# Fifteen of twenty 256 x 512 transposes of a two-layer mixer trunk moved from TensorE to VectorE block transposes and GpSimd copies

## The chip, the cores and the metric

One core of one Trainium2 chip runs the whole kernel in one launch. The metric is the device time of an execution in microseconds; lower is better. The kernel before has a median of 1819.05 us over three runs (1818.07 to 1819.42).

## What is computed

Two layers over x of 256 rows by 2048 columns, all in fp32. Cut to what matters here, a layer is:

```
h = rms_norm(x, norm_g)
p_sb, p_mla, p_rw, p_gate = split_cols(h @ w_in, ...)
y_sb  = stick_breaking_attention(...) * silu(sg)      # 256 x 512
y_mla = chunk_causal_softmax_attention(...) * silu(mg) # 256 x 1024
y_rw  = rwkv7_mixer(...) * silu(rg)                    # 256 x 512
g_sb, g_mla, g_rw = split_cols(sigmoid(p_gate), ...)   # 256 x 2048 each
merged = g_sb * (y_sb @ w_br_sb) + g_mla * (y_mla @ w_br_mla) + g_rw * (y_rw @ w_br_rw)
x = x + merged @ w_out
```

Every `@` with a weight needs its left operand with the columns on the partitions. So between the stages h, the gated branch outputs y and `merged` have to be transposed: per layer y in four pieces of 256 x 512, merged in four, and the new x in four before the next layer.

## The kernel before, in words

**Dense work.** The weights stream from HBM in chunks of 256 rows by up to 512 columns (0.5 MB), 280 chunks a layer in the fixed order of `GROUPS` (line 132). A chunk goes through four steps: SyncE loads it into one of four slots of `ring`; ScalarE (ACT) rounds it to `w_hi`; VectorE (DVE) writes the rest, `w_lo` = ring - w_hi; TensorE (PE) does twelve matmuls of 128 x 512 on it (hi x hi, hi x lo, lo x hi, for two halves of the rows and two blocks of 128) into one pair of the PSUM banks `D` (line 578). `LEAD` = 3: ACT and DVE split three chunks ahead of the one PE multiplies. `END[name]` is the number of chunks of a layer that are done when the group `name` ends; the groups near the change end at rg 184, gate11 192, mg0 200, mg1 208, sg 216, br0 218, bm0 222, bs0 224, then eight chunks for each next br/bm/bs trio, and o0 to o3 at 256, 264, 272 and 280.

**Order.** Every engine runs a program written out by hand. `dense_to(n)` emits an engine's share of the dense work up to chunk n, `beat()` the dense work up to the next step of the attention or RWKV work, which is laid between the chunks. Nothing is rescheduled: an engine that waits holds all that is behind it. DVE's share of the dense work holds the splits to `w_lo` and, in `take_out`, what becomes of a group's banks: the gating by SiLU (`rg`, `mg`, `sg`, which multiply `xy`), the merge (`br`, `bm`, `bs`, which build `MJ`) and the residual (`o`, which adds to `xy`).

**Transposes.** The four pieces of y are transposed by PE (line 632, function `transposes`) at `AT_RW` = mg1 + 2 chunks (the RWKV piece and the first MLA piece), `AT_ML1` = mg1 + 4 and `AT_SB` = after br0; the four pieces of merged by line 867 at `merged_at(j)`, three chunks after bs_j; the new x by line 632 at `renewed_at(j)`, two chunks after o_j, with the fourth piece two chunks into the next layer. A piece is eight transposes of 128 x 128 into two banks `B`. ACT then writes the rounded hi part from the bank and DVE the lo part, and PE's later matmuls wait for those (`br_dve`, `mt_dve`, `xt_dve`). With four pieces of y and four of merged in each layer, and four of x between the layers, that is twenty pieces.

**GpSimd (POOL)** masks the RWKV levels and the stick-breaking weights (`affine_select`, line 551, which PE waits for), spills the gates to HBM and reads them back three at a time (line 564), each read waiting until DVE has used the buffer.

## Time and profile before

| | |
|---|---|
| median of three runs | 1819.05 us |
| the profiled execution's own time | 1821.68 us |
| its span in the trace | 1819.9 us |
| granted TensorE clock, mean over the span | 0.997 of full speed |
| instructions | 22316 |
| HBM traffic over the span | 183 GB/s |

The profile is of one execution. Its times are from the span's start. "Busy" counts time in which an instruction of the engine runs; a matmul's end is modelled, so PE's next start says more than the duration of one. A line such as L1195 or L887 is that of a helper used for many things: the tile names tell them apart.

### The profile page before, as it was taken

The numbers are of one execution on the slowest core, as the hardware profiler recorded it, in microseconds if no ns is written. First come the engines' busy times: TensorE is split into PE (matmuls) and PEld (weight loads), VectorE is DVE, ScalarE is ACT, GpSimd is POOL, SyncE is SP. The second block draws the span as 40 slices with busy tenths as digits, with TensorE's granted clock in tenths as the row PEclk, the third lists the DMA queues.
The fourth block names the chain that finished last, engine by engine and source line by source line (L and its number), as shares of the span: only waits on it lengthen the run. The fifth ranks groups of instructions, "written<-read, shape, count | busy, mean of one in ns | idle before, by whom it ended". The sixth has DMA issues, their size and how long they took to land.

```text
span 1819.9 us, 22316 instructions
## 1 busy us (share of the span) xinstructions
PE 1778.6 (98%) x8912; PEld 1498.6 (82%) x8912; DVE 1074.2 (59%) x1388; ACT 880.7 (48%) x1234; POOL 138.9 (8%) x159
## 2 busy tenths in 40 slices
PE   6899999999999999999999999999999999999998
PEld 5678888889888888788888788888888888887887
DVE  3568454554866645686556774645557656467753
ACT  4444444334454666455544444434344555765532
POOL 1010111211000000100000010201100000001000
PEclk9999999999999999999999999999999999999999
DMA  7865555445565554785677655546456555558754
GB/s 235 237 192 177 173 159 165 149 143 170 174 187 154 165 152 153 258 281 181 208 231 236 188 164 154 170 139 183 135 168 193 160 159 159 150 174 309 238 188 155
DMA packets 178943, 335.19 MB, mean 184 GB/s; under 512 B 22556, under 2 KB 35258, under 8 KB 178168
## 3 DMA queue, kind: packets, MB, share of 16 engines
q1 hardware_dynamic: 169816, 297.67, 53.7%
q0 software_dynamic: 9024, 36.10, 5.6%
q8 instruction: 70, 1.15, 0.3%
q14 instruction: 33, 0.27, 0.0%
HBM read 313.56 MB, written 18.87 MB: 183 GB/s over the span
## 4 chain that ended last, share of the span: by engine, by line
PE 87%; DMA 4%; DVE 3%; ACT 3%; issue 1%; SPq 1%; ACTq 0%; DVEq 0%
PE D L578 73%; PE B L578 11%; DMA ring<-in_w_in 2%; DMA ring<-in_w_br_rw 2%; ACT arena L887 1%; DVE w_lo L1195 1%; DVE arena L1195 1%; ACT L887 1%; ACT w_hi L887 1%; PE B L632 0%; DVE xy L1195 0%; PE B L648 0%; PE B L867 0%; DMA xy<-in_x 0%; DVE gev L1233 0%
## 5 line engine op out<-in xcount | busy, mean ns | idle before, releaser
L1195 DVE TENSOR_TENSOR w_lo<-ring,w_hi 128x1024 fp32r<-128x1024 f32 (+3 forms) x560 | 661.7, 1195 | 457.0 <-ACT w_hi L887 448.5
L887 ACT ACTIVATE w_hi<-ring 128x1024 fp32r<-128x1024 f32 (+3 forms) x560 | 572.9, 1037 | 388.1 <-PE D L578 279.8
L578 PE MATMUL D<-w_hi,ht_hi 128*128 128x512 f32 (+2 forms) x1728 | 692.0, 400 | 16.4 <-DVE w_lo L1195 13.3
L578 PE MATMUL D<-w_hi,ht_lo 128*128 128x512 f32 (+2 forms) x1728 | 668.4, 387 | 0.0
L578 PE MATMUL D<-w_lo,ht_hi 128*128 128x512 f32 (+2 forms) x1728 | 666.8, 386 | 0.0
L578 PEld LDWEIGHTS D<-w_hi,ht_hi 128*128 128x128 f32 x1728 | 326.7, 189 | 80.4 <-DVE w_lo L1195 15.9
L578 PEld LDWEIGHTS D<-w_hi,ht_lo 128*128 128x128 f32 x1728 | 325.8, 189 | 67.3
L578 PEld LDWEIGHTS D<-w_lo,ht_hi 128*128 128x128 f32 x1728 | 327.0, 189 | 57.2 <-issue 0.5
L578 PEld LDWEIGHTS B<-arena 128*128 128x128 f32 (+3 forms) x1568 | 205.2, 190 | 24.6 <-issue 7.6
L578 PE MATMUL B<-arena 128*128 128x128 f32 (+5 forms) x1568 | 220.3, 293 | 1.4 <-DVE arena L1369 1.1
L887 ACT ACTIVATE arena<-B 128x512 f32<-128x512 f32 (+4 forms) x168 | 81.0, 491 | 286.7 <-PE B L578 229.3
L578 PE MATMUL D<-w_hi,mt_lo 128*128 128x512 f32 x256 | 100.5, 393 | 0.0
L578 PE MATMUL D<-w_hi,mt_hi 128*128 128x512 f32 x256 | 100.4, 392 | 0.0
L578 PE MATMUL D<-w_lo,mt_hi 128*128 128x512 f32 x256 | 100.1, 391 | 0.0
L526 POOL TENSOR_TENSOR arena<-arena,con 128x512 f32<-128x512 f32 x48 | 74.1, 1544 | 338.1 <-DVE arena L1308 185.8
L1195 DVE TENSOR_TENSOR arena<-arena,B 128x512 f32<-128x512 f32 x48 | 33.0, 687 | 59.5 <-PE B L578 59.5
L517 POOL DMA_DIRECT2D gate_spill<-gev x24 | 17.8, 743 | 636.9 <-ACT gev L887 636.9
L887 ACT ACTIVATE arena<-B,small 128x256 f32<-128x256 f32 (+1 forms) x48 | 20.8, 436 | 94.2 <-DVE small L1374 50.2
L887 ACT ACTIVATE arena<-arena 128x1024 f32<-128x1024 f32 (+4 forms) x72 | 54.0, 749 | 23.2 <-DVE small L1341 13.7
L1195 DVE TENSOR_TENSOR arena<-arena 128x1024 f32<-128x1024 f32 (+3 forms) x86 | 63.9, 751 | 1.8
L887 ACT ACTIVATE gev<-D,small 128x512 f32<-128x512 f32 (+1 forms) x64 | 40.4, 680 | 40.2 <-PE D L578 40.1
L578 PEld LDWEIGHTS D<-w_lo,mt_hi 128*128 128x128 f32 x256 | 48.1, 188 | 10.7
(135 smaller groups left out, 1276.7 us busy)
## 6 DMA issues: line engine op xcount, KB each, us to landing
ring<-in_w_in SPq DMA_DIRECT2D x368, 512.0 KB, 3.9
ring<-in_w_out SPq DMA_DIRECT2D x64, 512.0 KB, 4.8
ring<-in_w_br_mla SPq DMA_DIRECT2D x32, 512.0 KB, 4.7
gate_spill<-gev POOLq DMA_DIRECT2D x24, 512.0 KB, 4.2
arena<-gate_spill POOLq DMA_DIRECT2D x24, 512.0 KB, 4.9
ring<-in_mla_w_ukv SPq DMA_DIRECT2D x16, 512.0 KB, 4.1
ring<-in_w_br_rw SPq DMA_DIRECT2D x16, 512.0 KB, 6.4
ring<-in_w_br_sb SPq DMA_DIRECT2D x16, 512.0 KB, 5.3
```

What stands on the lines that cost most here:

```text
L517: pool.dma_start(spill[n].rearrange("(h p) c -> p h c", p=P), gev[:, n % 2, :, :]).then_inc(spilled[n % 2][l], 16)
L526: nc.gpsimd.tensor_tensor(LM, AM[:, :, 0:P], level[n].unsqueeze(1).to_broadcast([P, 4, P]), ALU.mult).then_inc(rw_pool, 1)
L578: return nc.tensor.matmul(o, a, b, start=start, stop=stop, skip_group_check=True)
L887: return nc.scalar.activation(o, i, fn, **kw)
L1195: return v.tensor_tensor(o, a, b, op)
```

## The change

For 15 of the 20 pieces, all but the stick-breaking piece and merged's fourth in each layer and x's fourth, PE's eight transposes go. In their place:

- **DVE** does one block transpose (`turn_blocks`) of the whole piece right after it has written it: each 32 x 32 block is transposed in place of itself, from `xy` or `MJ` into a new buffer `TURN` of 128 x 1024. The wait in front of it is for its own write, and for POOL to have emptied `TURN`.
- **POOL** then moves blocks between the four quarters of 32 partitions (`move`): sixteen `tensor_copy` of 32 partitions x 256 elements, four at a time with a wait behind each four, into `ROUND`. Three moves stand around the stick-breaking pairs, three between the gate reads, three at the end of layer 0.
- **ACT and DVE** read the hi and lo parts from `ROUND` in SBUF where they read banks `B`; ACT waits for `rows_moved`. `merged_at(j)` is now five chunks after bs_j (it was three), for j = 0 to 2, and `renewed_at(j)` four after o_j (it was two).

```diff
 def merged_at(j):
-    return END[f"br{j + 1}"] + 1 if j < 3 else END["bs3"] + 4
+    return END[f"bs{j}"] + (5 if j < 3 else 4)
 def renewed_at(j):
-    return END[f"o{j}"] + (2 if j < 3 else 0)
+    return END[f"o{j}"] + 4
...
+        TURN = [PV.rearrange("p h c -> p (h c)")[:, 0:1024]]
+        ROUND = [[PV.rearrange("p h c -> p (h c)")[:, (1 + n) * 1024:(2 + n) * 1024] for n in range(2)]]
...
+        def round_of(q):
+            return ROUND[q >= 3][q % 2].rearrange("p (k t) -> p k t", k=4)
...
+                def move(q):
+                    pool.wait_ge(blocks_turned[l], q + 1)
+                    turned = TURN[q >= 3].rearrange("p (h k j t) -> p h k j t", h=2, k=4, j=4)
+                    moved = round_of(q).rearrange("p k (h i t) -> p h k i t", h=2, i=4)
+                    for d in range(4):
+                        for i in range(4):
+                            j = (i + d) % 4
+                            nc.gpsimd.tensor_copy(moved[32 * j:32 * j + 32, :, :, i, :],
+                                                  turned[32 * i:32 * i + 32, :, :, j, :]).then_inc(quadrants[l], 1)
+                        pool.wait_ge(quadrants[l], 16 * q + 4 * d + 4)
+                    pool.sem_inc(rows_moved[l], 1)
...
                 dense_to(END["sv"])
+                move(0)
                 for q in range(SBH // 2):
...
+                    if q == 0:
+                        move(1)
                 dense_to(END["gate11"])
+                pool.wait_ge(br_dve[l], 2)
+                move(2)
...
+                    if n >= 5 and n % 3 == 2:
+                        j = n // 3 - 1
+                        if j:
+                            pool.wait_ge(mt_dve[l], 2 * j)
+                        move(3 + j)
+                for j in range(3 if l + 1 < DEPTH else 0):
+                    if j:
+                        pool.wait_ge(xt_dve[l], 2 * j)
+                    else:
+                        pool.wait_ge(mt_dve[l], 6)
+                    move(6 + j)
...
-                dense_to(AT_RW)
+                dense_to(AT_SB)
                 pe.wait_ge(sb_dve, 8 * l + 8)
-                pe.wait_ge(silu_dve[l], 6)
-                transposes((0, 1), 1536, br_pe[l])
-                transposes((2, 3), 512, br_pe[l])
-                dense_to(AT_ML1)
-                pe.wait_ge(br_dve[l], 2)
-                transposes((4, 5), 1024, br_pe[l])
-                dense_to(AT_SB)
-                pe.wait_ge(br_dve[l], 4)
                 pe.wait_ge(silu_dve[l], 8)
                 transposes((6, 7), 0, br_pe[l])
...
+            def turn_blocks(q, block):
+                if q:
+                    dve.wait_ge(rows_moved[l], q)
+                v.transpose(TURN[q >= 3].rearrange("p (h c) -> p h c", h=2), block).then_inc(blocks_turned[l], 1)
...
                     tt(y, y, gev[:, n % 2, :, :], ALU.mult).then_inc(silu_dve[l], 2)
+                    if n < 3:
+                        dve.wait_ge(silu_dve[l], 2 * n + 2)
+                        turn_blocks(n, y)
...
                         v.sem_inc(merged[l], 1)
+                        if j < 3:
+                            turn_blocks(3 + j, MJ[:, j % 2, :, :])
...
                     v.sem_inc(dense_ev[l], 1)
+                    if l + 1 < DEPTH and j < 3:
+                        turn_blocks(6 + j, xy[:, :, j * 512:(j + 1) * 512])
```

What each engine now issues, at the three places that matter most. First DVE where group rg of layer 0 is taken out, in the middle of MLA head 6: `xy<-xy,gev` is the gating of the RWKV piece, and the COPY is the head's rotary part, which PE waits for. Before:

```order
L1233 SCALAR_TENSOR_TENSOR gev<-arena,small,gev 128x64
L1195 TENSOR_TENSOR xy<-xy,gev 128x2x512 [waits dense_out_0]
L1369 COPY arena<-B 64x512 [waits ml_pe]
L1195 TENSOR_TENSOR w_lo<-ring,w_hi 128x1024 [waits weights_hi]
L1372 TENSOR_REDUCE small<-B 128x1 [waits ml_pe]
```

and now:

```order
L1274 SCALAR_TENSOR_TENSOR gev<-arena,small,gev 128x64
L1230 TENSOR_TENSOR xy<-xy,gev 128x2x512 [waits dense_out_0]
L1258 STREAM_TRANSPOSE arena<-xy 128x1024 [waits silu_gated_0]
L1415 COPY arena<-B 64x512 [waits ml_pe]
L1230 TENSOR_TENSOR w_lo<-ring,w_hi 128x1024 [waits weights_hi]
L1418 TENSOR_REDUCE small<-B 128x1 [waits ml_pe]
```

The block transpose stands between the gating and the copy; the rest is in the order it had.

Second, POOL between the two stick-breaking pairs of layer 0 (the first pair's masks end, the second pair's begin); before, the four masks followed each other. Now:

```order
L576 AFFINE_SELECT arena<-arena 128x128 [waits sb_act]
L576 AFFINE_SELECT arena<-arena 128x128
L561 COPY arena<-arena 32x2x4x32 [waits blocks_turned_0]
L561 COPY arena<-arena 32x2x4x32 x3
L561 COPY arena<-arena 32x2x4x32 [waits quadrants_moved_0]
...
L576 AFFINE_SELECT arena<-arena 128x128 [waits quadrants_moved_0,sb_act]
L576 AFFINE_SELECT arena<-arena 128x128
```

The second pair's masks stand behind a whole move, and behind its wait for DVE's block transpose.

Third, DVE from the end of bs0 in layer 0: `arena<-arena 128x1024` is the last addition of merged's first piece, `mt_lo` its lo part. Before:

```order
L1195 TENSOR_TENSOR arena<-arena 128x1024 [waits dense_out_0]
L1195 TENSOR_TENSOR w_lo<-ring,w_hi 128x1024 [waits dve_order,weights_hi]
L1195 TENSOR_TENSOR w_lo<-ring,w_hi 128x1024 [waits weights_hi]
L1195 TENSOR_TENSOR arena<-arena,D 128x512 [waits ring_freed,gate_sigmoid_0]
L1195 TENSOR_TENSOR arena<-arena,D 128x512
L1195 TENSOR_TENSOR w_lo<-ring,w_hi 128x1024 [waits dense_out_0,weights_hi]
L1195 TENSOR_TENSOR mt_lo<-B,mt_hi 128x512 [waits merged_hi_0] x2
```

and now:

```order
L1230 TENSOR_TENSOR arena<-arena 128x1024 [waits dense_out_0]
L1258 STREAM_TRANSPOSE arena<-arena 128x1024 [waits dve_order,rows_moved_0]
L1230 TENSOR_TENSOR w_lo<-ring,w_hi 128x1024 [waits weights_hi] x2
L1230 TENSOR_TENSOR arena<-arena,D 128x512 [waits ring_freed,gate_sigmoid_0]
L1230 TENSOR_TENSOR arena<-arena,D 128x512
L1230 TENSOR_TENSOR w_lo<-ring,w_hi 128x1024 [waits dense_out_0,weights_hi]
L1230 TENSOR_TENSOR w_lo<-ring,w_hi 128x1024 [waits weights_hi] x2
L1230 TENSOR_TENSOR mt_lo<-arena,mt_hi 128x512 [waits merged_hi_0] x2
```

The block transpose comes ahead of two splits, the lo part comes two splits later, and its input is `ROUND` where it was a bank.

## Rows read from the trace of the kernel before

**Rows 1.** The page: busy time by engine, and the chain's shares.

```profile
PE 1778.6 (98%) x8912; PEld 1498.6 (82%) x8912; DVE 1074.2 (59%) x1388; ACT 880.7 (48%) x1234; POOL 138.9 (8%) x159
...
PE 87%; DMA 4%; DVE 3%; ACT 3%; issue 1%; SPq 1%; ACTq 0%; DVEq 0%
```

**Rows 2.** Groups by line and shape: count, busy us, mean ns, idle before.

```profile
L632 PE MATMUL B<-con,xy 128*128 128x128 f32 x128 | 19.9, 311 | 9.9 <-DMA xy<-in_x 9.9
...
L867 PE MATMUL B<-con,arena 128*128 128x128 f32 x64 | 8.3, 273 | 0.0
```

**Rows 3.** PE's timeline around merged's first piece: start us, us, instruction.

```profile
774.27 0.40 PE L578 MATMUL D<-w_hi,ckv_lo 128*128 128x512 f32 x1
774.51 1.04 PE L867 MATMUL B<-con,arena 128*128 128x128 f32 x8
775.30 0.48 PE L578 MATMUL D<-w_hi,ckv_hi 128*128 128x512 f32 x1
775.61 0.39 PE L578 MATMUL D<-w_lo,ckv_hi 128*128 128x512 f32 x1
775.84 0.40 PE L578 MATMUL D<-w_hi,ckv_lo 128*128 128x512 f32 x1
```

**Rows 4.** The chain that ended last, in order of time, over the same place.

```profile
774.67 0.87 PE B L867 x8
775.54 21.80 PE D L578 x96
797.35 0.87 PE B L867 x8
```

**Rows 5.** Groups by line and shape on DVE.

```profile
L1195 DVE TENSOR_TENSOR w_lo<-ring,w_hi 128x1024 fp32r<-128x1024 f32 x512 | 618.6, 1222 | 412.9 <-ACT w_hi L887 404.6 <-DVE arena L1195 2.0 <-DVE small L1524 0.3
...
L1195 DVE TENSOR_TENSOR arena<-arena,D 128x512 f32<-128x512 f32 x48 | 30.8, 684 | 9.2 <-ACT arena L887 4.4 <-PE D L578 3.8 <-issue 1.1
...
L1323 DVE STREAM_TRANSPOSE arena<-arena 128x512 f32<-128x512 f32 x32 | 22.8, 712 | 1.1
```

**Rows 6.** DVE's and PE's timelines where rg is taken out, layer 0.

```profile
631.50 1.23 DVE L1195 TENSOR_TENSOR xy<-xy,gev 128x1024 f32<-128x1024 f32 x1
632.64 0.67 DVE L1369 COPY arena<-B 64x512 f32<-64x512 f32 x1
...
633.46 0.90 PE L578 MATMUL B<-arena 128*128 128x128 f32 x5 [0.42 <-DVE arena L1369]
```

**Rows 7.** DVE's timeline from bs0's merge on, layer 0.

```profile
771.15 1.23 DVE L1195 TENSOR_TENSOR arena<-arena 128x1024 f32<-128x1024 f32 x1
772.62 2.36 DVE L1195 TENSOR_TENSOR w_lo<-ring,w_hi 128x1024 fp32r<-128x1024 f32 x2 [0.24 <-DVE arena L1195]
774.89 1.28 DVE L1195 TENSOR_TENSOR arena<-arena,D 128x512 f32<-128x512 f32 x2
```

**Rows 8.** Groups by line and shape on POOL.

```profile
L526 POOL TENSOR_TENSOR arena<-arena,con 128x512 f32<-128x512 f32 x48 | 74.1, 1544 | 338.1 <-DVE arena L1308 185.8 <-PE B L578 152.3
...
L551 POOL TENSOR_SCALAR_AFFINE_SELECT arena<-arena 128x128 f32<-128x128 f32 x16 | 4.2, 291 | 90.6 <-ACT arena L887 90.6
...
L493 POOL MEMSET arena<- 1x256 f32 x4 | 1.2, 304 | 0.2
...
L493 POOL MEMSET arena<- 128x128 f32 x2 | 0.4, 212 | 0.1
```

**Rows 9.** POOL's and DVE's timelines, where both want SBUF.

```profile
407.55 2.09 POOL L526 TENSOR_TENSOR arena<-arena,con 128x512 f32<-128x512 f32 x1 [1.92 <-PE B L578]
...
187.19 1.31 POOL L526 TENSOR_TENSOR arena<-arena,con 128x512 f32<-128x512 f32 x1 [3.59 <-PE B L578]
...
406.17 2.32 DVE L1195 TENSOR_TENSOR w_lo<-ring,w_hi 128x1024 fp32r<-128x1024 f32 x2
409.07 1.65 DVE L1195 TENSOR_TENSOR w_lo<-ring,w_hi 128x1024 fp32r<-128x1024 f32 x1 [0.58 <-ACT w_hi L887]
```

**Rows 10.** ACT at merged's first piece; DVE, ACT and PE at x's first piece.

```profile
775.69 1.07 ACT L887 ACTIVATE mt_hi<-B 128x512 fp32r<-128x512 f32 x2
776.64 1.06 ACT L887 ACTIVATE w_hi<-ring 128x1024 fp32r<-128x1024 f32 x1
...
857.48 1.28 DVE L1195 TENSOR_TENSOR xy<-xy,D 128x512 f32<-128x512 f32 x2 [0.45 <-PE D L578]
...
863.95 1.57 ACT L887 ACTIVATE ht_hi<-B,small 128x256 fp32r<-128x256 f32 x4
...
857.21 0.39 PE L578 MATMUL D<-w_hi,mt_hi 128*128 128x512 f32 x1
```

**Rows 11.** Busy us by engine, clock, DMA share, GB/s: the merge's first two groups.

```profile
775.30:798.00 22.70, 22.70 (x108) 18.88 (x106) 19.05 (x21) 12.86 (x15) 2.89 (x4) 1.00 0.90 309
798.00:820.66 22.66, 22.66 (x108) 18.85 (x105) 17.22 (x18) 12.31 (x14) 1.44 (x2) 1.00 0.75 258
```

**Rows 12.** The second stick-breaking pair: gating on DVE, masks on POOL, PE's use.

```profile
690.88 1.23 DVE L1195 TENSOR_TENSOR xy<-xy,gev 128x1024 f32<-128x1024 f32 x1
...
706.61 1.03 POOL L551 TENSOR_SCALAR_AFFINE_SELECT arena<-arena 128x128 f32<-128x128 f32 x4 [28.39 <-ACT arena L887]
...
709.80 1.50 PE L578 MATMUL B<-arena 128*128 128x128 f32 x12
```

More of the change, by code:

```diff
@@ L275, in program @@
         CQ, CKV = again(at_mkv, lambda: halved(1024), lambda: halved(1024))
+        turn, round_ = again(at_mkv, lambda: take(1024), lambda: take(1024))
+        TURN.append(turn)
+        ROUND.append([round_, round_])
         KR = halved(128)
@@ L845, in _ @@
                     sb_pair(q)
-                dense_to(AT_RW)
+                dense_to(AT_SB)
                 pe.wait_ge(sb_dve, 8 * l + 8)
-                pe.wait_ge(silu_dve[l], 6)
-                transposes((0, 1), 1536, br_pe[l])
-                transposes((2, 3), 512, br_pe[l])
-                dense_to(AT_ML1)
-                pe.wait_ge(br_dve[l], 2)
-                transposes((4, 5), 1024, br_pe[l])
-                dense_to(AT_SB)
-                pe.wait_ge(br_dve[l], 4)
                 pe.wait_ge(silu_dve[l], 8)
                 transposes((6, 7), 0, br_pe[l])
-                for j in range(4):
-                    dense_to(merged_at(j))
-                    pe.wait_ge(merged[l], j + 1)
-                    for s in range(2):
-                        if j:
-                            pe.wait_ge(mt_dve[l], 2 * j - 1 + s)
-                        for k in range(2):
-                            for h in range(HALVES):
-                                kk = 2 * s + k
-                                last = nc.tensor.transpose(B[s][:, k * 256 + h * P:k * 256 + (h + 1) * P],
-                                                           MJ[:, j % 2, h, kk * P:(kk + 1) * P], ident)
-                        last.then_inc(mt_pe[l], 1)
-                for j in range(3 if l + 1 < DEPTH else 0):
-                    dense_to(renewed_at(j))
-                    pe.wait_ge(x_new[l], j + 1)
-                    if j < 2:
-                        pe.wait_ge(mt_dve[l], 8)
-                    else:
-                        pe.wait_ge(xt_dve[l], 2 * j - 2)
-                    transposes((2 * j, 2 * j + 1), j * 512, xt_pe[l])
+                dense_to(merged_at(3))
+                pe.wait_ge(merged[l], 4)
+                for s in range(2):
+                    for k in range(2):
+                        for h in range(HALVES):
+                            kk = 2 * s + k
+                            last = nc.tensor.transpose(B[s][:, k * 256 + h * P:k * 256 + (h + 1) * P],
+                                                       MJ[:, 1, h, kk * P:(kk + 1) * P], ident)
+                    last.then_inc(mt_pe[l], 1)
                 dense_to(NCH)
@@ L1070, in sb_pair, with columns_hi @@
                 beat()
-            def columns_hi(j, ready, done):
+            def columns_hi(j, ready, done, before=0):
                 for s in (2 * j, 2 * j + 1):
-                    act.wait_ge(ready, s + 1)
+                    act.wait_ge(ready, s + 1 - before)
                     for i in range(2):
@@ L1079, in columns_hi, with renewed_hi @@
                     last.then_inc(done, 1)
+            def renewed_hi(j):
+                act.wait_ge(rows_moved[l], 7 + j)
+                for s in (2 * j, 2 * j + 1):
+                    for i in range(2):
+                        k = 2 * s + i
+                        last = f(hth[:, k, :], round_of(6 + j)[:, k % 4, :], scale=ng[:, k:k + 1])
+                    last.then_inc(xt_act[l], 1)
             def squares(j, done):
@@ L1428, in columns_lo, with renewed_lo @@
                     last.then_inc(done, 1)
+            def renewed_lo(j):
+                for s in (2 * j, 2 * j + 1):
+                    dve.wait_ge(xt_act[l], s + 1)
+                    for i in range(2):
+                        k = 2 * s + i
+                        last = v.scalar_tensor_tensor(htl[:, k, :], round_of(6 + j)[:, k % 4, :], ng[:, k:k + 1],
+                                                      hth[:, k, :].bitcast(F32), ALU.mult, ALU.subtract)
+                    last.then_inc(xt_dve[l], 1)
             def sum_squares(squared, done):
```

63 lines of the change are left out of this document (36 added, 27 removed).

## The prediction

> **What bounds the kernel now.** I read the page's busy times and the chain first [rows 1]. PE is busy 98% of the span and 87% of the chain that ended last is PE; DVE is at 59%, POOL at 8%. So an instruction taken off PE shortens the run, unless it stood in the shadow of a wait. The groups by line say whether the transposes did [rows 2]: before the 64 of line 867 PE never sat idle, and all 9.9 us before line 632 are waits for the input x at the start, which stay. The 120 transposes that go (15 pieces of eight) were therefore paid in full. Then I read the places where work is put in: DVE and PE around rg [rows 6], DVE after bs0 [rows 7], POOL between the stick-breaking pairs [rows 12], and the prices of what is added [rows 5, 8, 9].
>
> **What goes.** A transpose's row says 273 ns, but they overlap: eight run from 774.51, and the dense matmuls go on at 775.30, the next at 775.61 [rows 3]. From 774.27 to 775.61 are 1.34 us; two matmul intervals of 0.227 us (96 in 21.80 us [rows 4]) would have stood there anyway, which leaves 0.89 us for eight. The chain gives 0.87 twice [rows 4]. 15 x 0.89 = **13.4 us**. The stick-breaking piece, merged's fourth and x's fourth stay on PE, at no change.
>
> **What DVE gets.** Fifteen block transposes of 128x1024. The trace has them of 128x512, at 712 ns, beside 684 ns for an elementwise instruction of that size and 1222 ns for one of twice the size [rows 5]. By that slope a block transpose of twice the size takes 712 + 538 = 1.25 us, and 15 take 18.8 us of an engine with 41% idle. Where is one on the path?
> - *rg, once a layer.* PE waits 0.42 us for the COPY that DVE does right after the gating [rows 6]. The block transpose now stands between them. Nothing covers it: 1.25 us and 0.05 for the wait on the gating, twice = **+2.6 us**.
> - *bs0, once a layer.* DVE was held up by late weights here. Its pair of splits starts at 772.62, and the first of them, done at 773.84, is what PE's matmuls from 775.30 need [rows 3, 7]. Without the transposes PE wants it at 774.5; the block transpose (from 772.5 to 773.75) pushes it to 775.0. PE waits 0.5, twice = **+1.0 us**.
> - *Everywhere else* (mg0, mg1, bs1, bs2, o0 to o2) DVE works ahead of PE. In the group from bs1 to bs2 it is busy 17.2 of 22.66 us [rows 11]; with the block transpose 18.5 of the new 21.8. Cost 0; without that cover each would be 1.3 us.
>
> **What POOL gets.** Sixteen copies a piece, of 32 partitions x 256 elements. The trace has no POOL copy. Nearest below: a memset of 256 elements on few partitions, 304 ns. Nearest above with one input and one output: an affine select of 128 elements, 291 ns, twice that for 256 = 582 ns [rows 8]. From 128 to 256 elements a memset grows by 92 ns, so I take 291 + 92 = 383 ns for a copy, and keep both ends. The four waits of a move cost some 0.05 us each.
>
> POOL also gets in DVE's way and DVE in POOL's. A POOL instruction that takes 1.31 us alone took 2.09 when it met DVE's split of `w_lo`; the next split, which wanted to start while POOL was running, took 1.65 instead of 1.22 [rows 9]. So the two exclude each other while both read SBUF, and either may lose. The Trainium skill says the same (SBUF — State Buffer, "SBUF: two separate sides"): the shared port pair is an exclusive lock held for the whole instruction, against DVE instructions with two SBUF inputs too. By that rule, the trace agrees, all DVE splits and additions count, and the lo parts, which read a PSUM bank before and SBUF now, join them. During a move DVE has about two splits to do, 2.4 us. A move takes **T = 16c + 0.2 + 2.4**: 8.7 us at c = 0.383, 7.5 at 0.304, 11.9 at 0.582.
>
> Where does T reach PE? ACT waits for the moved rows, and with it the splits behind it; PE has three chunks in hand.
> - *Merged's first piece.* Turned at 773.75. After the move ACT's hi parts take 1.07 us, the next split 1.06 on ACT and 1.22 on DVE, the emptying of bm1's banks 1.28 [rows 5, 7, 10]: 4.6 us. PE wants that five chunks after 775.0, at 2.725 us a chunk (12 matmuls) = 788.6. T may be **10.2**.
> - *Merged's second and third.* Turned about 4.3 us after the next group starts (1.28 + 1.22 + 1.25 and 0.5 of waits), wanted 21.8 us after it: T may be **12.9**.
> - *x's pieces.* Turned at 857.48 + 1.28 + 1.35 = 860.1; then 1.57 + 1.06 + 1.22 + 0.1; wanted seven chunks of 2.745 after 857.21 = 876.4 [rows 10]. T may be **12.4**.
> - *The second stick-breaking pair.* The gating ends at 692.1, so the move starts at 693.4 and must be over, with 1.03 us of masks behind it, by PE's use at 709.80 [rows 12]: T may be **15.4**.
> - *The pieces of y.* rg's has 40 us to its use at mg1 + 2, mg1's has its use at the end of sg, some 16 us later.
>
> At 8.7 none is reached, and the move costs nothing but DVE's waits for POOL. Those count only where DVE is late, after bs0: between nothing and the four queued copies of a step (1.5 us) a layer. I take one copy, 0.4: **+0.8 us**.
>
> **Sum.** -13.4 + 2.6 + 1.0 + 0.8 = -9.0. The profiled execution took 1821.7, so 1812.7; the median of the runs is 2.6 lower than it, so **1810.1**. The bounds of the unknown terms: full gain (nothing lost at rg or bs0) -13.4, 1805.7; with the four queued copies (+2.2 more) and c at 0.582 (T 11.9, 1.7 over at merged's first piece, twice = 3.4) 1815.7.
>
> **Rivals.**
> 1. *The copies are slow, and the kernel gets slower.* For it: no row shows a copy between quarters of the partitions, and POOL's two-input instruction takes 1544 ns for 512 elements [rows 8], 0.77 for 256. At c = 0.77, T = 14.9: over the limit by 4.7 twice, 2.0 four times, 2.5 three times = 24.9 us; 1810.1 + 24.9 = 1835.0. Against it: a copy has one input, and part of the 1544 is waiting for DVE (1.31 undisturbed [rows 9]). It decides from T = 13.1, c = 0.66, where the stalls (5.8 + 0.8 + 2.1) eat the 9 us. The Trainium skill speaks for it (GPSIMD Engine Reference, "Key points"): only two of the eight cores reach all partitions, so such work runs at a quarter of the engine. If that quadrupled only the 92 ns per 128 elements, c would be 0.66, an estimate at the turning point itself. Chance 0.14.
> 2. *DVE becomes the bound in the merge.* 18.5 us of 21.8, and if it waits for all sixteen copies (6.1 us), 24.6: 2.8 over for six groups, less the some 5 us that each layer's three chunks in hand absorb: about 6.8 us. 1810.1 + 6.8 = 1816.9. For it: DVE did lose to POOL in rows 9; against it: it also won there. Chance 0.10.
> 3. *Weights, not PE.* The DMA of the chunks bounds the merge (309 and 258 GB/s in its first two groups [rows 11]), so that its six pieces give nothing: 1810.1 + 5.3 = 1815.4. Against: PE never idles there. Chance 0.05.
> 4. *rg costs nothing*, since PE waits elsewhere in the MLA chain anyway: 1807.5. Chance 0.08.
>
> Forecast as summed: 0.63.
>
> **Numbers.** Some 0.2% (3.6 us) is what a measurement of this kernel can tell from no change, so faster means under 1815.4. The forecast, the fourth rival and about half of the second and third lie there: 0.63 x 0.97 + 0.08 + 0.08 = 0.77. Same, up to 1822.7: the rest of those and a slow copy near the turning point: 0.11. Slower: 0.12. The range 1805.5 to 1818 takes in the bounds and rivals 2 to 4 and leaves out the slow copies, and a little on either side.
>
> **What would show it.** Right: transposes on PE down by 120; PE's gap at the COPY in MLA head 6 near 1.7 us instead of 0.42; a gap near 0.5 after bs0; the block transposes at 1.25 us; POOL's moves at 7 to 10 us, over before ACT reaches its read; groups of 21.8 us in the merge. Wrong: ACT's idle time before `mt_hi` put down to POOL with PE idle behind it (rival 1); `w_lo` well over 1.22 us and PE waiting for it in several groups (rival 2); ACT waiting for the ring with PE idle (rival 3).

## The result and the profile after

The changed kernel took 1825.84 us (median of five runs, 1822.58 to 1828.28), 1.0036 times the kernel before (95% interval 1.0024 to 1.0049). On another chip it took 1824.18 us (seven runs) beside 1819.60: 1.0027 (1.0016 to 1.0037). It is slower, by 4.6 to 6.8 us, where 9 us less were forecast.

The page of the changed kernel, against [rows 1]:

```profile
PE 1770.3 (97%) x8792; PEld 1486.0 (82%) x8792; DVE 1095.3 (60%) x1403; ACT 878.5 (48%) x1234; POOL 286.7 (16%) x399
...
PE 85%; DVE 6%; ACT 3%; DMA 3%; issue 2%; POOL 1%; SPq 0%; DVEq 0%; ACTq 0%; POOLq 0%
```

The transposes did go (120 instructions, 8.3 us of busy time), and POOL's busy time doubled; but DVE's share of the chain doubled too, and POOL appears in it. The groups by line on DVE and POOL, against [rows 5, 8]:

```profile
L1230 DVE TENSOR_TENSOR w_lo<-ring,w_hi 128x1024 fp32r<-128x1024 f32 x512 | 621.8, 1231 | 378.6 <-ACT w_hi L906 371.6 <-DVE arena L1230 0.5 <-DVE small L1579 0.3
...
L1258 DVE STREAM_TRANSPOSE arena<-xy 128x1024 f32<-128x1024 f32 x9 | 11.2, 1245 | 0.7
...
L561 POOL COPY arena<-arena 32x256 f32<-32x256 f32 x240 | 147.9, 616 | 136.2 <-DVE arena L1258 86.9 <-DVE cq_lo L1230 36.0
```

The block transpose takes 1.245 us, as forecast. A copy's mean of 616 ns is of two kinds: most take 0.39 us and some 1.3. Where TensorE waits is in the summary of its waits:

```profile
PE D L618 <- DVE arena L1230: 12.7, 8, 2.5
...
PE B L618 <- DVE arena L1415: 3.6, 2, 1.9
```

"arena" from line 1230 is the emptying of a pair of banks D. Eight long waits for it: one at br1 in each layer, which the kernel before has as well, and six new ones in the merge. Line 1415 is rg's COPY. The merge by windows, each from one group's first matmul to the next's (br1 to br2, to br3, to o0), against the 22.70 and 22.66 us of [rows 11]; the columns are us, busy us of PE, PEld, DVE, ACT and POOL with instructions in brackets, granted clock, DMA share, GB/s:

```profile
760.01:784.08 24.07, 22.35 (x97) 17.86 (x97) 18.52 (x20) 12.25 (x14) 12.94 (x19) 1.00 0.74 241
784.08:808.13 24.05, 22.37 (x97) 17.86 (x97) 18.73 (x20) 12.03 (x14) 12.84 (x19) 1.00 0.71 241
808.13:832.18 24.05, 22.41 (x96) 17.86 (x96) 18.68 (x20) 12.02 (x14) 12.13 (x18) 1.00 0.69 219
```

A group was to take 21.8 us and takes 24.05, in both layers: 6 x 2.25 = 13.5 us. No engine is full (PE 22.4, DVE 18.7, POOL 12.8), DMA moves less than before and the clock is 1.00. That is the picture of a loop of waits that is longer than any engine's work. One turn of it, by the timelines of DVE, POOL, ACT and PE (start us, us, instruction, idle before and its releaser):

```profile
780.13 1.29 DVE L1230 TENSOR_TENSOR mt_lo<-arena,mt_hi 128x512 fp32r<-128x512 f32 x2 [4.63 <-ACT mt_hi L906]
781.60 1.22 DVE L1230 TENSOR_TENSOR w_lo<-ring,w_hi 128x1024 fp32r<-128x1024 f32 x1 [0.18 <-ACT w_hi L906]
782.75 1.28 DVE L1230 TENSOR_TENSOR arena<-arena,D 128x512 f32<-128x512 f32 x2
784.06 1.23 DVE L1230 TENSOR_TENSOR arena<-arena 128x1024 f32<-128x1024 f32 x1
785.43 2.36 DVE L1230 TENSOR_TENSOR w_lo<-ring,w_hi 128x1024 fp32r<-128x1024 f32 x2
787.71 1.28 DVE L1230 TENSOR_TENSOR arena<-arena,D 128x512 f32<-128x512 f32 x2
789.02 1.23 DVE L1230 TENSOR_TENSOR arena<-arena 128x1024 f32<-128x1024 f32 x1
790.49 1.25 DVE L1258 STREAM_TRANSPOSE arena<-arena 128x1024 f32<-128x1024 f32 x1 [0.25 <-DVE arena L1230]
791.66 2.52 DVE L1230 TENSOR_TENSOR w_lo<-ring,w_hi 128x1024 fp32r<-128x1024 f32 x2
...
791.88 11.55 POOL L561 COPY arena<-arena 32x256 f32<-32x256 f32 x16 [0.55 <-DVE arena L1258]
...
792.90 0.50 PE L618 MATMUL D<-w_hi,ckv_hi 128*128 128x512 f32 x1 [0.35 <-DVE w_lo L1230]
...
803.51 1.15 ACT L906 ACTIVATE mt_hi<-arena 128x512 fp32r<-128x512 f32 x2 [4.52 <-POOLq L564]
...
804.18 1.29 DVE L1230 TENSOR_TENSOR mt_lo<-arena,mt_hi 128x512 fp32r<-128x512 f32 x2 [3.72 <-ACT mt_hi L906]
...
808.13 0.50 PE L618 MATMUL D<-w_hi,cq_hi 128*128 128x512 f32 x1 [1.33 <-DVE arena L1230]
```

Read it as a circle. At 780.13 DVE starts `mt_lo` of one piece. Behind it in DVE's order stand a split, the emptying of bm1's banks, two splits, the emptying of bs1's banks with the merge, and the next block transpose, done at 791.74: 11.6 us of DVE work, nearly back to back. Then POOL moves for 11.55 us, and 0.1 later ACT writes the first `mt_hi`, so that the next `mt_lo` starts at 804.18. 11.6 + 11.7 + 0.75 = 24.05. TensorE is not in the circle: it hangs on it by bm's banks, emptied only behind `mt_lo`. The next group's first matmul waits 1.3 us for them and starts 1.5 us late (the group's last chunk takes 4.2 us where an undisturbed one takes 2.72). Most of what is left of the 2.25 us, 0.65, comes at the group's third and fourth chunks, where a split stands behind the block transpose and TensorE sits idle for 0.35 us (792.90).

The move itself is longer than forecast. The chain in order of time has four copies of the next move; the last line is a split of DVE in the move above:

```profile
815.93 1.23 POOL arena L561
817.21 1.28 POOL arena L561
818.55 0.39 POOL arena L561
...
819.00 0.41 POOL arena L561
...
799.02 1.44 DVE L1230 TENSOR_TENSOR w_lo<-ring,w_hi 128x1024 fp32r<-128x1024 f32 x1 [0.81 <-ACT w_hi L906]
```

Undisturbed copies start 0.45 us apart (16 x 0.45 = 7.2); five of the sixteen are held up by a DVE split and take some 0.88 us more. DVE loses too: the split at 799.02 started 0.03 us after a copy and took 1.44 us in place of 1.22, and the copy behind it took 1.28. That both engines lose by turns is what the rows of before showed [rows 9]. The Trainium skill's rule (SBUF — State Buffer, "SBUF: two separate sides") is a lock on the shared ports, held for the whole instruction; these rows agree with it.

At rg, against [rows 6], the block transpose stands between gating and COPY, and TensorE waits 1.67 us where it waited 0.42 (1.91 for 0.66 in layer 1):

```profile
629.77 1.25 DVE L1258 STREAM_TRANSPOSE arena<-xy 128x1024 f32<-128x1024 f32 x1
630.94 0.64 DVE L1415 COPY arena<-B 64x512 f32<-64x512 f32 x1
...
631.73 0.46 PE L618 MATMUL B<-arena 128*128 128x128 f32 x2 [1.67 <-DVE arena L1415]
```

### The profile page after: what moved, and what is told of

The parts are those of the page before. It is cut to its first block, busy times and chain, and to the rows that moved or that the text cites. A ratio compares the mean times of both kernels' runs of the same rounds, so it can differ in the third digit from the quotient of the medians.

```text
span 1820.8 us, 22347 instructions
## 1 busy us (share of the span) xinstructions
PE 1770.3 (97%) x8792; PEld 1486.0 (82%) x8792; DVE 1095.3 (60%) x1403; ACT 878.5 (48%) x1234; POOL 286.7 (16%) x399
## 4 chain that ended last, share of the span: by engine, by line
PE 85%; DVE 6%; ACT 3%; DMA 3%; issue 2%; POOL 1%; SPq 0%; DVEq 0%; ACTq 0%; POOLq 0%
PE D L618 71%; PE B L618 11%; DVE arena L1230 2%; DVE w_lo L1230 1%; ACT arena L906 1%; DMA ring<-in_w_in 1%; ACT L906 1%; DMA ring<-in_w_br_rw 1%; ACT w_hi L906 1%; POOL arena L561 1%; DMA ring<-in_w_br_mla 1%; DVE xy L1230 0%; PE B L688 0%; DVE gev L1274 0%; ACT gev L906 0%
## 5 line engine op out<-in xcount | busy, mean ns | idle before, releaser
L618 PE MATMUL D<-w_hi,ht_hi 128*128 128x512 f32 (+2 forms) x1728 | 692.4, 401 | 12.9 <-DVE w_lo L1230 9.8
L561 POOL COPY arena<-arena 32x256 f32<-32x256 f32 x240 | 147.9, 616 | 136.2 <-DVE arena L1258 86.9
L906 ACT ACTIVATE arena<-arena 128x1024 f32<-128x1024 f32 (+4 forms) x72 | 53.9, 749 | 23.1 <-DVE small L1387 13.8
```

The source lines that it names most:

```text
L561: nc.gpsimd.tensor_copy(moved[32 * j:32 * j + 32, :, :, i, :], turned[32 * i:32 * i + 32, :, :, j, :]).then_inc(quadrants[l], 1)
L618: return nc.tensor.matmul(o, a, b, start=start, stop=stop, skip_group_check=True)
L906: return nc.scalar.activation(o, i, fn, **kw)
```

## The experiments

The theories as they stood: **A**, the loop just read is the loss, and it breaks if the piece is read later or moved faster. **B**, DVE is the bound in the merge, whatever POOL does. **C**, the loss lies in stretches of a lower granted clock. Later C was split: **D**, such stretches follow idle gaps of TensorE of 1.6 us and more, of which the change makes more; **E**, they don't, or the first measurement was of a poor hour.

Two numbers are given of each kernel: the median beside that of the kernel before on the same chip, and the time in the profile from the first matmul of the 17th chunk to the last matmul ("behind the start"). The second leaves out the first 65 to 69 us, which differ by up to 3.8 us from one profile to the next with the arrival of the first weights, and so it is the sharper one, though of one execution only. It is 1746.5 us for the kernel before. "Stretches" counts the times in it that TensorE was granted 1.2 GHz instead of 2.4. One stretch costs 1.6 us: the br1 group's first two chunks in v1_both_mends, beside the same two in the changed kernel without one:

```profile
759.57:766.77 7.20, 7.20 (x25) 5.75 (x25) 6.78 (x7) 4.75 (x5) 1.40 (x2) 0.76 0.77 259
```
```profile
760.01:765.58 5.57, 5.57 (x25) 4.61 (x25) 5.39 (x6) 4.45 (x5) 0.72 (x1) 1.00 0.74 241
```

| kernel | median | before beside it | ratio, 95% interval | behind the start | stretches | less 1.63 each |
|---|---|---|---|---|---|---|
| before | | | | 1746.5 | 1 | 1744.9 |
| changed, first | 1825.84 | 1819.05 | 1.0036 (1.0024, 1.0049) | 1750.2 | 2 | 1747.0 |
| changed, again (c0) | 1824.18 | 1819.60 | 1.0027 (1.0016, 1.0037) | 1749.3 | 3 | 1744.4 |
| e1 merged on TensorE | 1818.48 | 1819.61 | 0.9996 (0.9988, 1.0005) | 1743.4 | 3 | 1738.5 |
| e2 half the copies | 1810.37 | 1819.61 | 0.9949 (0.9936, 0.9961) | 1738.3 | 2 | 1735.1 |
| e3 read two chunks later | 1813.41 | 1819.61 | 0.9966 (0.9954, 0.9979) | 1738.4 | 2 | 1735.1 |
| e4 rg's turn later | 1819.06 | 1819.61 | 0.9998 (0.9989, 1.0007) | 1746.7 | 1 | 1745.1 |
| e5 read one chunk later | 1812.46 | 1820.44 | 0.9956 (0.9943, 0.9970) | 1739.8 | 4 | 1733.3 |
| e6 before, with rg's turn | 1825.36 | 1819.60 | 1.0038 (1.0024, 1.0052) | 1750.8 | 2 | 1747.6 |
| v1 = e3 + e4 | 1809.28 | 1819.60 | 0.9950 (0.9937, 0.9962) | 1736.1 | 3 | 1731.2 |
| v1 again | 1808.33 | 1820.44 | 0.9935 (0.9923, 0.9947) | 1734.0 | 2 | 1730.7 |
| v2 = e1 + e4 | 1814.83 | 1819.60 | 0.9971 (0.9962, 0.9980) | 1739.9 | 2 | 1736.6 |
| v3 = v1, read eight later | 1808.69 | 1820.44 | 0.9936 (0.9923, 0.9948) | 1735.4 | 3 | 1730.5 |
| v4 = v1, gaps filled | 1806.33 | 1820.44 | 0.9924 (0.9910, 0.9937) | 1731.8 | 0 | 1731.8 |
| v4 again | 1805.72 | 1819.00 | 0.9930 (0.9916, 0.9944) | 1731.7 | 0 | 1731.7 |
| e7 before, gaps filled | 1817.44 | 1819.00 | 0.9993 (0.9985, 1.0002) | 1744.8 | 0 | 1744.8 |
| e8 changed, gaps filled | 1821.24 | 1819.00 | 1.0014 (1.0005, 1.0023) | 1747.7 | 0 | 1747.7 |

The last column takes off too much where a stretch falls right after br1 in a kernel whose merged pieces are moved. TensorE would have waited there anyway, some 0.7 us in the mended kernels and nearly the whole 1.6 us in the changed one. That is so for two stretches each in c0, e5, v1, v1 again and v3 and for one in e2.

### The merge loop

**e1_merge_on_pe.** merged's three pieces a layer go back to TensorE; the pieces of y and x stay moved.

```diff
 def merged_at(j):
-    return END[f"bs{j}"] + (5 if j < 3 else 4)
+    return END[f"br{j + 1}"] + 1 if j < 3 else END["bs3"] + 4
...
-                        if j < 3:
-                            turn_blocks(3 + j, MJ[:, j % 2, :, :])
...
```

> merged's pieces are turned by TensorE again, as before the change; nine of the fifteen pieces stay moved. A (in the merge the way from a turned piece to its halves has grown longer than a group of blocks): the six merge groups lose their stall of 2.25 us each and pay 0.89 us of transposes each again, so 9 x 0.89 = 8.0 us are gained against the kernel before and rg's block transpose costs 2.6: about 5.4 us below before, 1813.7. B (VectorE is the bound in the merge, whoever turns the block): the period of a merge group goes back to 22.68 us too, so B gives the same here. C (the loss is in stretches of a lower granted clock, wherever they come, and not in the merge): nothing changes against the changed kernel, 1824 to 1827.

The groups are back at 22.82 and 22.66 us (24.41 for the one with a stretch in it), so the loss in the merge is of the moved pieces. The median is only 1.1 us below before, not 5.4. The rows behind the start, though, give 1738.5 against 1744.9 without the stretches: 6.4 less, near the counted 5.5. What was missing are two more stretches than before had.

**e2_half_copies.** The last two of the four rounds of copies are left out for merged's pieces, so half of each of these blocks holds old values.

```diff
-                    for d in range(4):
+                    for d in range(2 if 3 <= q < 6 else 4):
...
-                        pool.wait_ge(quadrants[l], 16 * q + 4 * d + 4)
+                        pool.wait_ge(quadrants[l], 16 * q - 8 * min(max(q - 3, 0), 3) + 4 * d + 4)
```

> Of merged's three moved pieces only 8 of the 16 partition quarters are moved, so half of each such block of merged^T holds old values; all else is as in the changed kernel. A: the move takes about 5.9 us in place of 11.7, the closed loop of 24.05 us becomes at most 18.2, below the group of 21.8, so no group stalls for it: 6 x 2.25 = 13.5 us less than the changed kernel, about 1812. B (what VectorE has to do in a group, block transpose and splits and merge, is what fills it): the copies hold up VectorE's splits half as often, five stretched splits of 0.15 us become two or three, so at most 6 x 0.5 = 3 us, about 1823. C: 1824 to 1827.

1810.37, as A said; B's 1823 is refuted. Eight copies take 7.06 us (four of them held up), and the group 21.76, against 24.05, with DVE busy for 19.17 us of it, more than in the changed kernel:

```profile
787.58 7.06 POOL L561 COPY arena<-arena 32x256 f32<-32x256 f32 x8 [0.55 <-DVE arena L1258]
...
782.79:804.55 21.76, 21.76 (x97) 18.02 (x96) 19.17 (x20) 12.39 (x13) 8.81 (x11) 1.00 0.84 283
```

**e3_read_later.** ACT and DVE read each moved piece of merged two chunks later.

```diff
 def merged_at(j):
-    return END[f"bs{j}"] + (5 if j < 3 else 4)
+    return END[f"bs{j}"] + (7 if j < 3 else 4)
```

> merged's moved pieces are read seven blocks after bs_j in place of five, so two blocks later; every instruction stays. A: the loop gets two blocks (3.6 us) more before TensorE wants the piece, 24.05 against 21.8 + 3.6 = 25.4 allowed, so the groups run at 21.8 to 22.3 us: 10 to 13.5 us less than the changed kernel, 1812 to 1816. B: the group is as long as VectorE's work in it, the wait only moves to another block: 1824 to 1827. C: the same.

1813.41, in A's range, with every instruction still there. The move even got longer, 14.3 us: eight of its copies are held up, by seven splits and an addition. The first group has no wait for bm's banks left, but still the one behind the block transpose:

```profile
763.22:785.78 22.56, 22.21 (x97) 18.05 (x98) 19.95 (x19) 11.03 (x12) 14.98 (x18) 1.00 0.77 257
```

**e5_read_one_later.** The same with 6 for 7. The point of it: is the piece's way of fixed length, or a circle through DVE's order?

> merged's moved pieces are read six blocks after bs_j, between the five of the changed kernel and the seven of e3_read_later. If the way of a piece is fixed at 24.05 us and TensorE's group sets the allowance (21.8 + 1.8), the stall is 0.45 per group: 1815 to 1818. If the loop runs over VectorE (mt_lo of a late piece stands ahead of the work that ends in the next block transpose), the period is the move, mt_hi, and what VectorE does between mt_lo and the next block transpose, whatever TensorE does: one fewer operation group behind mt_lo gives 22.5 us or less per group, 1814 to 1817. Neither gives 1824.

Groups of 21.76 us and a median of 1812.46, below both ranges. The time does not decide between the two: the expectation reckoned 1.8 us for one chunk, but a chunk takes 2.72 us (twelve matmuls), so a way fixed at 24.05 us would have fitted into 21.8 + 2.7 as well. DVE's timeline shows what one chunk did:

```profile
780.68 1.28 DVE L1230 TENSOR_TENSOR arena<-arena,D 128x512 f32<-128x512 f32 x2
782.00 1.23 DVE L1230 TENSOR_TENSOR arena<-arena 128x1024 f32<-128x1024 f32 x1
784.24 1.29 DVE L1230 TENSOR_TENSOR mt_lo<-arena,mt_hi 128x512 fp32r<-128x512 f32 x2 [1.01 <-ACT mt_hi L906]
785.71 2.36 DVE L1230 TENSOR_TENSOR w_lo<-ring,w_hi 128x1024 fp32r<-128x1024 f32 x2 [0.17 <-ACT w_hi L906]
787.98 1.28 DVE L1230 TENSOR_TENSOR arena<-arena,D 128x512 f32<-128x512 f32 x2
789.30 1.23 DVE L1230 TENSOR_TENSOR arena<-arena 128x1024 f32<-128x1024 f32 x1
790.77 1.25 DVE L1258 STREAM_TRANSPOSE arena<-arena 128x1024 f32<-128x1024 f32 x1 [0.25 <-DVE arena L1230]
...
792.15 12.45 POOL L561 COPY arena<-arena 32x256 f32<-32x256 f32 x16 [0.55 <-DVE arena L1258]
```

bm1's banks are now emptied ahead of the wait for the moved piece (780.68) and not behind it. So TensorE gets them in time, and between `mt_lo` (784.24) and the end of the next block transpose (792.02) are 7.8 us in place of 11.6. The circle is shorter by those 3.8 us, more than the move of 12.45 us gives back. The piece's own way did not get shorter: from a group's first matmul to the start of `mt_lo` it is 20.1 us in the changed kernel (784.08 to 804.18) and 20.4 here (785.84 to 806.20). That the loop runs through DVE's order, and not through TensorE, rests on the changed kernel's rows, where DVE goes from `mt_lo` to the block transpose with hardly a pause; no run tests that alone.

**v3_read_eight_later.** v1 (below) with 8 for 7.

> v1_both_mends with merged's moved pieces read eight blocks after bs_j instead of seven. If seven is still at the edge of the loop (groups of 21.83 to 21.90 us in e3, 21.76 in e2), eight gains up to 0.1 us per group, 0.6 in all, which the measurement can't tell: 1808 to 1810. If at eight blocks the next piece's move has to wait for mt_lo (the moved block has one place), the groups grow again: 22 us or more, 1811 or more.

1808.69: no different from v1 again (1808.33) by these measurements. The moved block's one place did cost POOL a wait (1.25 us before each next move), but nothing waited for POOL.

### rg, and the clock

**e4_rg_turn_later.** rg's block transpose moves from `take_out` to behind the MLA heads.

```diff
-                    if n < 3:
+                    if n in (1, 2):
...
                 dense_to(END["sv"])
+                dve.wait_ge(silu_dve[l], 2)
+                turn_blocks(0, xy[:, :, 1536:2048])
```

> rg's block transpose (1.245 us on VectorE) stands behind the MLA heads, no longer ahead of the COPY of MLA head 6 that TensorE waits for; all else is as in the changed kernel. Under every theory of the merge the two gaps of 1.67 and 1.91 us on TensorE go back to 0.42 and 0.66: 2.5 us less than the changed kernel, 1823.3. If instead the COPY was late for another reason, the gaps stay and the time too. C says also that a lower-clock stretch that comes behind such a gap may go with it.

TensorE's gaps are 0.42 and 0.65 again, and the six merge groups still take 24.06 to 24.15. The median is 6.8 below the changed kernel's first and 5.1 below c0's, both on other chips; 2.5 was counted, so by the medians another 2.6 to 4.3 us went with the gaps, as C had said might happen. The profiles show less: behind the start e4 is 3.5 us below the first and 2.5 below c0. Of the 6.0 us between c0's profiled execution and e4's, 3.5 lie ahead of the 17th chunk, where the first weights arrive.

**c0_changed_again.** No edit.

> The changed kernel once more, on the chip and beside the runs of the three others. D (what is beyond the counted gaps is 1.6 us for every stretch that TensorE is granted 1.2 GHz, and such stretches come behind idle gaps of TensorE of 1.6 us and more, of which this kernel has two more than rg_turn_later): 1822 to 1828, and 2.5 us plus up to 3.3 us above e4_rg_turn_later. E (the first measurement of it was of another chip or another hour): about 1821.5, the 1819.06 of e4_rg_turn_later plus 2.5 and nothing more.

1824.18: the loss is real, and E's 1821.5 is below all but one of its seven runs, though not by much. Of c0's three stretches two fall right after br1, where TensorE would have had to wait for the merge loop anyway (24.12 us for that group instead of 24.07); that is why its last column is too low.

```profile
764.66:788.78 24.12, 23.67 (x97) 19.07 (x97) 18.53 (x20) 12.38 (x14) 12.99 (x19) 0.93 0.73 241
```

**e6_before_rg_turn.** The kernel before, with rg's block transpose alone, into a spare tile.

```diff
                     tt(y, y, gev[:, n % 2, :, :], ALU.mult).then_inc(silu_dve[l], 2)
+                    if n == 0:
+                        dve.wait_ge(silu_dve[l], 2)
+                        spare = PV.rearrange("p h c -> p (h c)")[:, 0:1024]
+                        link(v.transpose(spare.rearrange("p (h c) -> p h c", h=2), y))
```

> The kernel before with one thing added: a block transpose of rg's block into a spare tile on VectorE (1.245 us) ahead of the COPY in MLA head 6, once in each layer; nobody reads it, nothing is moved. TensorE's gap there becomes 1.68 and 1.91 us. E: +2.5 us, ratio 1.0014, 1822.1. D: +2.5 and for each layer up to one stretch at 1.2 GHz of 1.6 us: +2.5 to +5.8, about 1824.

5.8 us slower for two instructions of 1.25 us. Behind the start the profile is 4.3 us longer: some 2.7 us for the two gaps (1.82 and 2.06 us in place of 0.42 and 0.66), and one stretch more, behind the second of them. E's 2.5 us is below the interval (1.0024 times before is 4.4 us more); D's upper end fits.

**v2_merge_on_pe_rg_turn_later.** e1 with e4's edit.

> e1_merge_on_pe with rg's block transpose behind the MLA heads: nine pieces moved, 9 x 0.89 = 8.0 us less of TensorE than before, no merge stall, no gap at rg. e1 came out only 1.1 us below before where its chunk starts give 8.0 - 2.5 = 5.5. D: the missing 4.4 us are lower-clock stretches behind rg's gap; with the gap gone they go too, so 1819.6 - 8.0 = 1811.6, at most 1813. E: the missing part stays: 1818.5 - 2.5 = 1816.

1814.83, above D's limit of 1813 and below E's 1816. The rows behind the start show the counted 8 us (8.3 without the stretches). Its two stretches come behind gaps that every kernel has. So removing rg's gap did not remove all of e1's: D is right in kind only if the other large gaps count as well. The count over 13 profiles (before, changed twice, e1 to e6, v1 twice, v2, v3), behind the first 100 us: TensorE has 66 idle gaps of 1.67 to 3.07 us (rg where the block transpose precedes the COPY, mg0's fifth chunk, br1's first), and 30 of them are followed within 1.6 us by a stretch at 1.2 GHz: 5 of the 14 at rg, 12 of the 26 at mg0, 13 of the 26 at br1. It has 55 gaps of 0.9 to 1.6 us, the merge loop's 1.3 us among them, and none is. There are 30 stretches in all, so none comes elsewhere. Which of the large gaps it strikes changes from run to run of the same kernel.

**v4_filled, v4_again.** v1 with those gaps filled by transposes of the identity into a bank nobody reads.

```diff
+            def fill(bank, count):
+                for _ in range(count):
+                    nc.tensor.transpose(bank[:, 0:P], ident, ident)
...
+                        if name == "br1" and c == 0:
+                            fill(B[0], 20)
+                        if name == "mg0" and c == 4:
+                            pe.wait_ge(dense_ev[l], gi)
+                            fill(banks(l, gi + 1)[0], 14)
```

> v1_both_mends, and in each layer TensorE's two idle gaps of over 1.6 us (1.81 at mg0's fifth chunk, 2.65 and 2.93 at br1's first) are filled by 14 and 20 transposes of the identity into banks that nobody reads, 0.111 us each, so that TensorE starts the next chunk no earlier than before. D (a lower-clock stretch follows some of the idle gaps of over 1.6 us): no stretch at 1.2 GHz in the profile between the first 100 us and the last 10, and up to three of 1.65 us less: 1804.5 to 1807.5. If the stretches come at their moments whatever TensorE did before: the time of v1_again, and the profile shows them. If the fillers outlast the gaps: slower than v1_again by their excess.

> v4_filled again: 1804 to 1808. Against e7_before_filled the counted difference is that of v1: 13.4 us of transposes and up to 0.5 us back, so 12.9 to 13.4 us below e7.

No stretch is left behind the start. Around br1 in TensorE's timeline, v1_both_mends and then v4_filled:

```profile
759.57 0.50 PE L618 MATMUL D<-w_hi,cq_hi 128*128 128x512 f32 x1 [2.65 <-DVE arena L1230]
...
760.74 0.63 PE L618 MATMUL D<-w_lo,cq_hi 128*128 128x512 f32 x1
```
```profile
756.41 2.35 PE L623 MATMUL B<-con 128*128 128x128 f32 x20
758.82 0.50 PE L618 MATMUL D<-w_hi,cq_hi 128*128 128x512 f32 x1
...
759.38 0.40 PE L618 MATMUL D<-w_hi,cq_lo 128*128 128x512 f32 x1
```

In v1 the matmuls take 0.63 us 1.2 us after the gap; in v4 they stay at 0.39 to 0.40. The medians are 1806.33 and 1805.72 against 1808.33 and 1809.28, 2.0 to 3.6 us less. Where v4_filled and v1_again ran beside each other it was 2.0, with runs that overlap; D's range of 1804.5 to 1807.5 holds both medians.

**e7_before_filled, e8_changed_filled.** The same filling in the kernel before, and in the changed kernel, there with 13 transposes at rg as well.

> The kernel before, its two idle gaps of over 1.6 us in each layer (1.80 at mg0's fifth chunk, 2.35 and 2.52 at br1's first) filled with 14 and 20 transposes of the identity. D (lower-clock stretches follow such gaps): one stretch per run less on average, 1.65 us: 1817 to 1819, and none in the profile behind the first 100 us. If the stretches come whatever TensorE does: the time of the kernel before.

> The changed kernel with the same two gaps filled, and rg's (1.67 and 1.91 us) with 13 transposes of the identity; the merge loop of 24.05 us and rg's late COPY stay. D: what is left over e7_before_filled are the counted differences alone: 15 transposes less, 6 x 2.25 us of merge stalls, 2.5 us at rg, together +2.2: 1819 to 1821, and none of the stretches at 1.2 GHz behind the first 100 us. If the loss beyond the counted 2.2 us has another cause: 4 us or more above e7, 1823 to 1825.

No stretch behind the start in either, and both fell: before by 1.6 us (within its interval of nothing), the changed kernel to 1821.24. Their difference is 3.8 us, 2.9 by the rows behind the start (1747.7 to 1744.8), of which 0.6 come at the start of layer 1, where profiles differ by as much without a cause in the change. The expectation was 2.2 and a changed kernel at 1821 at most, its rival 4 or more. The medians don't tell these apart, since their difference is good to some 2 us either way; by the rows it is the first. Without filling the difference was 4.6 to 6.8, so by the medians the clock carries one to three microseconds of the changed kernel's loss, which is about what their intervals allow for.

The granted clock of every run says more. One stretch is some 0.001 of its mean over the span. That mean is 0.996 to 0.997 for the kernel before (68 runs on four chips), 0.994 for the changed kernel's first five runs and 0.995 for c0's seven, 0.995 for e6 (five), 0.996 for e4 (eleven), and 0.998 for e7 and e8 (eleven each). So the changed kernel has one to three stretches more than before in an average run, and the filled kernels have fewer than either.

### Both mended

**v1_both_mends, v1_again.** e3's and e4's edits together.

> e3_read_later and e4_rg_turn_later together. By the starts of TensorE's chunks: 15 transposes less, 13.4 us, no merge stall, no gap at rg, and 0.2 us per layer at the moved pieces: e3's profiled run without the two 1.25 us. D: e3_read_later 1813.4 minus 2.5 and minus up to 3.3 for the lower-clock stretches behind those gaps: 1808 to 1811. E: 1813.4 minus 2.5, 1810.9, with nothing below 1810. If the two edits meet on VectorE and eat each other's gain: above 1811.5.

> v1_both_mends again, beside the next three on their chip: 1808 to 1811.

1809.28 and 1808.33, 0.9950 and 0.9935 times before, and below E's floor of 1810: two small edits of place bring the change to where the forecast had it. What is counted of it is 13.4 us for the transposes less 1.6 in the first merge groups (22.56 for 21.76, twice), 11.8. By the rows behind the start without the stretches 13.7 and 14.2 us are gained, or 12.4 and 12.8 when 0.7 is given back for each stretch right after br1. The pair without stretches, v4 again against e7 on one chip, has 13.0 us by the rows and 11.7 by the medians (1817.44 to 1805.72), where 12.9 to 13.4 was expected. The 1.2 us that these rows have over 11.8 lie at the start of layer 1 (0.2) and from bs0's to br1's first matmul in layer 1 (1.0), a part of the kernel that takes 7.5 to 8.8 us from one profile to another.

## Why the prediction was wrong

**Right.** The price of a transposed piece, 0.89 us: merge groups take 22.66 us with the transposes and 21.76 without (e5), x's groups 22.86 and 21.97, and y's three pieces give 2.67. The block transpose at 1.25 us: 1.245. rg: 1.25 us a layer, TensorE's gap 1.67 where "near 1.7" was written. After bs0 0.5 was forecast and 0.36 came, in both layers, and with POOL's lock the two small terms made 1.8 of the sum; e3's first merge group, at 22.56 over 21.76 in each layer, has 1.6. x's and y's pieces cost nothing. A copy alone: 0.39 us for 0.383. The Trainium skill's sentence that a kernel which has to reach all partitions runs at a quarter of the engine's cores (GPSIMD Engine Reference, "Key points"), on which the estimate of 0.66 us rested, does not show in this copy. The first rival (slow copies, slower from T = 13.1) named the right sign for the wrong reason, and its turning point was never reached. The third and fourth did not come: none of TensorE's long waits in the merge is put down to weights, and rg's gap grew by the whole 1.25 us.

**Wrong, first step: T and its limit in the merge.** The limit for merged's first piece was right: T came out at 11.7 (11.72 in the trace) over a limit of 10.2, and that group is 24.07 against e3's 22.56, 1.5 late. Two numbers failed behind it.
- T = 16c + 0.2 + 2.4 = 8.7 counted about two DVE splits in a move. Five fell into it, and each held a copy for 0.88 us: 4.4 us. The sixteen copies themselves, 0.45 apart and not 0.383 + 0.0125, came to 7.2. Two small misses made 3 us.
- The limit of 12.9 for the second and third piece assumed that each piece is turned 4.3 us after its group starts. e2, with short moves, has 4.65. The changed kernel has 7.66, since once the first piece is late, DVE does bm's emptying, three splits and bs's emptying behind it. A limit for a repeating group has to be that of the circle: T + 0.75 + 11.6 may be at most 21.8, so T may be **9.4**, not 12.9. T was over it by 2.3, six times.

Both misses were needed. With T at 8.7 the circle would have been 21.05 us, inside the group's 21.8. With T at 11.7 the prediction's own limits give 1.5 us twice at merged's first piece and nothing at the other four, 3 us in all, and not the 12 us that the six groups cost beyond the 1.8 in the sum.

The second rival had the place and nearly the size (24.6 us a group, against 24.05) and a mechanism akin to it, DVE held up in the merge; it went wrong in making DVE's amount of work the bound (e2 shows that it isn't) and in taking off 5 us a layer for the three chunks in hand: against e3's groups the changed kernel loses 1.5 us in a layer's first and 2.2 in each of the next two, so nothing like 5 us was absorbed.

**Wrong, second step: an idle gap was priced at its length.** TensorE's gap at rg was lengthened from 0.42 to 1.67, over the size from which the clock sometimes falls. The sum took the difference, 1.25 us. The rows show 1.6 us more behind 30 of 66 such gaps, so a gap carried over that size costs about 0.7 us on the mean beyond its length, 1.5 for the two (1.2 by rg's own 5 of 14), and up to 3.3 in a single run.

**The sum redone** with what the rows show: -13.4 + 2.5 (rg) + 13.8 (six groups, 144.3 us for 130.6) = +2.9. The rows behind the start have +2.1 without the stretches and +3.7 with them, and e8 against e7, with none, +2.9. Half a microsecond to either side lies at the start of layer 1, ahead of rk: the changed kernel's profile is 0.5 ahead of before's there, but so is e7's, which has nothing of the change, and e8's is 0.6 behind e7's. The medians have 4.6 and 6.8; the profile that goes with the first is of its fastest run (1822.58), and the other four had a mean granted clock of 0.991 to 0.995 against 0.997 in that one. By that they had two to six stretches more, some of which may lie in the first 65 us; there is no profile of them.

**Open.** Why 30 of the 66 gaps and not the others is not settled: they don't order by length (1.67 to 3.07 us) or by place. Nor is it shown how much of the 4.6 to 6.8 us between the medians is clock and how much scatter: 2.9 us is counted, and one to three stretches more a run at 1.6 us each would bring it to 4.5 to 7.7, but stretches were counted in two profiles of the changed kernel only.

## What to carry to other kernels

When work is taken off the bound engine and given to others in a loop, draw the circle: start at the wait, list everything that stands behind it on its engine up to the instruction that starts the next turn, add the transfer, and compare the total with the period, not the piece's way with the slack of one turn. If it is too long, a wait moved one chunk later in the waiting engine's order can be worth as much as half the transfer (groups of 21.76 us in e5 and in e2), because it takes other work out of the circle. And count the held-up instructions of a shared port from the timeline of the whole stretch (what the other engine does in the transfer's lengthened time), not from its undisturbed time.

## What the runs showed of the hardware

- A POOL copy of 32 x 256 fp32 elements from one quarter of the partitions to another takes 0.39 to 0.41 us, 0.45 from start to start, for each of the sixteen pairs of quarters; when it starts during a DVE instruction with two inputs in SBUF it takes 1.22 to 1.30 us (58 of the 62 held up in the changed kernel). The loss goes both ways: splits that started during a copy took 1.35 to 1.45 us instead of 1.22.
- TensorE's granted clock can fall to 1.2 GHz after an idle gap of as little as 1.68 us (e5, at rg) in otherwise dense work (30 of 66 gaps of 1.67 to 3.07 us, none of 55 between 0.9 and 1.6), at 1.6 us a time. Filling such gaps with matmuls that nobody reads kept the clock at 2.4 GHz behind the start in all four profiles.
- While the clock was low right ahead of a stall, it cost nearly nothing: c0's merge group with a stretch in it took 24.12 us, the same group without one 24.07.
